# Two stages of a hybrid layer become one block: the whole output product in 32 units of pieces, with a ring of weight slots

## What is computed

```
attn = sliding_window_attention(q, k, v, sinks) * silu(z_attn)
...
y = ssd_chunked(xs, dt, a, bm, cm)
y = y + (xs.reshape(b, l, N_SSM_HEADS, SSM_HEAD_DIM) * d_skip[:, None]).reshape(b, l, D_INNER)
ssm = gated_rmsnorm(y, z_ssm, ssm_norm_w)
out = jnp.einsum("ble,ed->bld", jnp.concatenate([attn, ssm], axis=-1), w_out)
return layer_norm_2(DEEPNORM_ALPHA * x + out, ln_g, ln_b)
```

## Time and profile before

| | us |
|---|---|
| median of 3 runs | 3448.87 (3447.88 to 3450.91) |
| profiled execution, its own time | 3451.71 |
| its span, first to last instruction | 3449.8 |
| layer 0: state-space block | 2146.2 to 2400.4 |
| layer 0: `state_out_and_norm`, last product | 2400.4 to 2498.05 |
| layer 1: the same | 3087.1 to 3341.5, 3341.5 to 3439.9 |
| mean granted TensorE clock | 0.953 |

### The profile page before, as it was taken

The page is one execution under the profiler, slowest core; times in us unless marked ns, Lnnn a source line. Parts: engine busy times, 40 slices in busy tenths (PEclk is TensorE's granted clock), DMA queues, the critical chain, the costliest instruction groups (busy, mean ns, idle before and its releaser), DMA issues. The chain is left out here.

```text
span 3449.8 us, 49680 instructions
## 1 busy us (share of the span) xinstructions
PE 3145.1 (91%) x21066; PEld 2491.3 (72%) x21066; DVE 1482.6 (43%) x2152; ACT 1061.8 (31%) x1832; POOL 996.3 (29%) x658
## 2 busy tenths in 40 slices
PE   5998799785999998998999998788999999978888
PEld 3886498674888887887777776566777777756667
DVE  3999644434222224342243342554412433425544
ACT  3012333323222222222243443541213444444411
POOL 2443022103333323322333332221323333321212
PEclk8999799897999999999999999899999999988999
DMA  5113300122111111123111222653331112226432
GB/s 199 49 49 116 105 4 4 44 100 93 47 48 49 49 36 52 60 95 100 50 61 62 74 86 91 217 147 104 114 86 50 62 62 74 92 104 204 144 113 102
DMA packets 296327, 292.82 MB, mean 85 GB/s; under 512 B 10784, under 2 KB 252832, under 8 KB 291648
## 3 DMA queue, kind: packets, MB, share of 16 engines
q1 hardware_dynamic: 252320, 235.28, 21.5%
q10 hardware_dynamic: 43808, 54.66, 4.6%
HBM read 233.16 MB, written 54.66 MB: 83 GB/s over the span
## 5 line engine op out<-in xcount | busy, mean ns | idle before, releaser
L1880 PE MATMUL PS<-x_high_sb,w_high_sb 128*128 128x512 f32 x1312 | 530.1, 404 | 0.0
L1880 PE MATMUL PS<-x_high_sb,w_low_sb 128*128 128x512 f32 x1312 | 518.2, 395 | 0.0
L1880 PE MATMUL PS<-x_low_sb,w_high_sb 128*128 128x512 f32 x1312 | 517.4, 394 | 0.0
L1880 PEld LDWEIGHTS PS<-x_high_sb,w_high_sb 128*128 128x128 f32 x1312 | 246.9, 188 | 76.1 <-issue 23.9
L1880 PEld LDWEIGHTS PS<-x_high_sb,w_low_sb 128*128 128x128 f32 x1312 | 246.8, 188 | 57.8
L360 PE MATMUL PS<-h_high_sb,up_high_sb 128*128 128x512 f32 x704 | 274.7, 390 | 14.1 <-POOL up_low_sb L1445 14.1
L1880 PEld LDWEIGHTS PS<-x_low_sb,w_high_sb 128*128 128x128 f32 x1312 | 247.3, 188 | 52.4
L360 PE MATMUL PS<-h_low_sb,up_high_sb 128*128 128x512 f32 x704 | 274.6, 390 | 0.0
L360 PE MATMUL PS<-h_high_sb,up_low_sb 128*128 128x512 f32 x704 | 274.4, 390 | 0.0
L1495 DVE SCALAR_TENSOR_TENSOR z_sb<-PS,cols_sb,z_sb 128x1023 f32<-128x1023 f32 x88 | 112.8, 1282 | 348.5 <-ACT z_sb L1476 342.1
L2118 DVE CUSTOM_DVE_ANT_0 scores_sb<-PS,alibi_sb,sinks_sb 128x256 f32<-128x256 f32 (+1 forms) x256 | 104.4, 465 | 342.5 <-PE PS L1898 342.5
(11 more groups left out here) (414 smaller groups left out, 6316.6 us busy)
## 6 DMA issues: line engine op xcount, KB each, us to landing
w_raw_sb<-w_in SPq DMA_DIRECT2D x102, 512.0 KB, 3.8
up_raw_sb<-w_up SPq DMA_DIRECT2D x44, 512.0 KB, 3.8
ada_slots_sb<-ada_w SPq DMA_DIRECT2D x16, 1024.0 KB, 5.9
attn_raw_sb<-attn ACTq DMA_DIRECT2D x32, 512.0 KB, 4.7
decays_sb<-running_sums SPq DMA_DIRECT2D x16, 1024.0 KB, 5.2
w_raw_sb<-w_out SPq DMA_DIRECT2D x64, 256.0 KB, 3.5
xbc<-staged_sb ACTq DMA_DIRECT2D x24, 512.0 KB, 2.6
xbc_sb<-xbc SPq DMA_DIRECT2D x16, 768.0 KB, 6.9
```

Source lines behind the costliest of these rows:

```text
L1880: last = pe.matmul(PS[:, bank, :], a[:, n % 2, k], b[:, k, cols], start=k == 0 and a is WH and b is HH, stop=k == KT - 1 and a is WL)
```

## The change

The two blocks become one, `state_space_and_mix`. The output product has 32 units in four parts of 8: attention rows with the left columns, attention rows with the right columns, ssm rows left, ssm rows right. Units 0 and 1 run ahead of chunk 0, two units in each chunk, units 18 and 19 around the last norm, and 20 to 31 behind it. Units 0 to 17 share one PSUM bank, the later ones take four in turn. The ssm units read y from HBM in the same layout as the attention units. The weights of all 32 pieces pass through a ring of 11 slots (`WS`), and a slot is filled again when the last unit of a part has used its piece (`slot_empty`). The first 8 pieces are loaded into the room of y and state by two transfers and split by ScalarE and VectorE (`first`) at the block's start; pieces 8 to 31 are split by GpSimd, in three runs between the `grow` passes. SyncE issues pieces 10 to 12 in chunk 1, 13 to 20 in chunk 2, 21 to 26 in chunk 6, and the last 5 into the room of y and state. The z gate has one buffer where it had two, so `gates(c)` waits for `gate(c - 1)`. The squares go to y's own room. The norm weight is multiplied in `normalise`, now 8 passes of 128 columns. The layer norm is what it was.

```diff
@@ -2175,7 +2175,9 @@
-def state_space_and_attention_out(m, d_skip, xbc_d, gate_d, rows_d, attn_d, y_d, src, w, DT, A, NA, EI, DE, CD):
+def state_space_and_mix(m, layer, d_skip, xbc_d, gate_d, rows_d, attn_d, y_d, src, w, ln_g, ln_b, dst, ahead,
+                        DT, A, NA, EI, DE, CD):
...
@@ -2183,34 +2185,39 @@
-    SLOTS = 3
-    UNITS = 2 * TT
+    SLOTS, WS = 3, 11
+    UNITS, FREE = 4 * TT, 2 * TT + 2
...
-        ZS = alloc(m, ctx, "z_gate", [P, 2, KT, P])
+        ZS = alloc(m, ctx, "z_gate", [P, KT, P])
...
+        YS = alloc(m, ctx, "y_and_state", [P, 4, DI])
...
+        WH = alloc(m, ctx, "w_high", [P, WS, NH], F32R)
+        WL = alloc(m, ctx, "w_low", [P, WS, NH], F32R)
+        Y, S = YS[:, 0:2], YS[:, 2:4]
+        raw = YS[:].rearrange("p a (b n) -> p (a b) n", n=NH)
...
@@ -2218,6 +2225,23 @@
+        bank = lambda u: OUT if u < FREE else (u - FREE) % 4
+        before = lambda u: u if u < FREE else u - 3
+        LATE, RESIDUAL = [4, 5, 6, 7, 0], [0, 1, 4, TT]
+        late = lambda i: i - (4 * KT - len(LATE))
...
+        def slot_empty(eng, i):
+
+            j, q = (i - WS) // KT, (i - WS) % KT
+            if q == KT - 1:
+                eng.wait_ge(s.prod, TT * (j + 1))
+            else:
+                eng.wait_ge(s.piece, (KT - 1) * j + q + 1)
@@ -2232,42 +2256,46 @@
...
             def gates(c):
-                sp.dma_start(ZS[:, c % 2], chunk(gate_d[:, :, cols(c)])).then_inc(z_in[c % 2], 16)
+                if c:
+                    sp.wait_ge(s.gate, c)
+                sp.dma_start(ZS[:], chunk(gate_d[:, :, cols(c)])).then_inc(s.z_in, 16)
...
+            def first_weights(i):
+                sp.dma_start(raw[:, 4 * i:4 * i + 4], w[4 * i * P:4 * (i + 1) * P, 0:NH].rearrange("(q p) n -> p q n", p=P)
+                             ).then_inc(first_in[i], 16)
+
+            def piece_of(i):
+                part, q = i // KT, i % KT
+                row, half = part // 2 * KT + q, part % 2
+                return w[row * P:(row + 1) * P, half * NH:(half + 1) * NH]
 
             def weights(i):
-                if i >= 2:
-                    sp.wait_ge(s.wsplit, i - 1)
-                half, q = i // KT, i % KT
-                sp.dma_start(RAW[:, i % 2], w[q * P:(q + 1) * P, half * NH:(half + 1) * NH]).then_inc(raw_in[i % 2], 16)
+                if i >= KT + 2:
+                    sp.wait_ge(s.wsplit, i - KT - 1)
+                sp.dma_start(RAW[:, i % 2], piece_of(i)).then_inc(raw_in[i % 2], 16)
 
             def store(c):
                 sp.wait_ge(s.normed, c + 1)
                 sp.dma_start(chunk(y_d[:, :, cols(c)]), YT[:, c % 2]).then_inc(y_out[c % 2], 16)
 
             inputs(0)
+            sp.dma_start(skip[:], d_skip.to_broadcast([P, SH])).then_inc(s.skip_in, 16)
+            first_weights(0)
+            first_weights(1)
+            residual(0)
             rows(0)
-            weights(0)
-            weights(1)
-            sp.dma_start(skip[:], d_skip.to_broadcast([P, SH])).then_inc(s.skip_in, 16)
+            residual(1)
             rows(1)
-            weights(2)
             inputs(1)
-            weights(3)
-            residual(0)
-            weights(4)
-            rows(2)
-            weights(5)
-            gates(0)
-            weights(6)
-            residual(1)
-            weights(7)
-            gates(1)
             weights(8)
             weights(9)
+            rows(2)
+            gates(0)
+            residual(2)
             for c in range(TT):
                 sp.wait_ge(s.yd, c + 1)
-                if c == 4:
-                    for i in range(10, 2 * KT):
-                        weights(i)
+                for i in {1: range(10, 13), 2: range(13, 21), 6: range(21, 27)}.get(c, ()):
+                    weights(i)
                 if c:
                     store(c - 1)
-                    if c + 1 < TT:
-                        gates(c + 1)
+                    gates(c)
+            sp.wait_ge(s.yo, TT - 1)
+            sp.wait_ge(s.ss, TT - 1)
+            for i in range(4 * KT - len(LATE), 4 * KT):
+                sp.dma_start(raw[:, LATE[late(i)]], piece_of(i)).then_inc(s.tail_in, 16)
+                if i == 4 * KT - len(LATE):
+                    store(TT - 1)
...
@@ -2294,19 +2331,23 @@
+                    i = u // TT * KT + q
                     if q == 0:
                         pe.wait_ge(s.low, u + 1)
-                        if u:
-                            pe.wait_ge(s.added, u)
+                        if u and before(u):
+                            pe.wait_ge(s.added, before(u))
                     if k == 0:
-                        pe.wait_ge(s.wsplit, half * KT + q + 1)
+                        if i < KT:
+                            pe.wait_ge(s.wfirst, i + 1)
+                        else:
+                            pe.wait_ge(s.wsplit, i - KT + 1)
...
@@ -2396,80 +2438,106 @@
 
             b_and_cb(0)
             x_turned(0)
+            fill(2 * KT)
             for c in range(TT):
-                n = 1 if c else 0
                 if c + 1 < TT:
                     b_and_cb(c + 1)
-                fill(n)
+                fill(1)
                 if c:
                     from_state(c)
-                else:
-                    fill(4)
-                fill(2 * n)
+                fill(2)
                 if c < TT - 1:
                     to_state(c)
                 fill(2)
                 if c:
                     y_turned(c - 1)
-                fill(2 * n)
+                fill(2)
                 within(c)
-                fill(1 if c else 2)
+                fill(1)
                 if c + 1 < TT:
                     x_turned(c + 1)
-                fill(3 * n)
+                fill(3)
                 if c:
                     square_sums(c - 1)
-                fill(3 * n)
+                fill(3)
                 if c:
                     spread(c - 1)
-                fill(2 * n)
+                fill(2)
             y_turned(TT - 1)
-            fill(4)
+            pe.wait_ge(s.xde, TT)
+            fill(KT)
             square_sums(TT - 1)
-            fill(4)
+            fill(KT)
             spread(TT - 1)
+            fill(len(pieces))
...
             def split(i):
-                half, q = i // KT, i % KT
...
+                if late(i) >= 0:
+                    pool.wait_ge(s.tail_in, 16 * len(LATE))
+                    piece = raw[:, LATE[late(i)]]
+                else:
+                    pool.wait_ge(raw_in[i % 2], 16 * (i // 2 - KT // 2 + 1))
+                    piece = RAW[:, i % 2]
+                if i >= WS:
+                    slot_empty(pool, i)
+                nc.gpsimd.tensor_copy(WH[:, i % WS], piece).then_inc(s.wchain, 1)
+                pool.wait_ge(s.wchain, i - KT + 1)
+                nc.gpsimd.tensor_tensor(WL[:, i % WS], piece, WH[:, i % WS], ALU.subtract).then_inc(s.wsplit, 1)
...
-                if c == 5:
-                    for i in range(KT, 2 * KT):
-                        split(i)
+
+            pool.wait_ge(s.wfirst, KT)
+            for i in range(KT, WS):
+                split(i)
+            for c in range(1, 4):
+                grow(c)
+            for i in range(WS, WS + KT):
+                split(i)
+            for c in range(4, TT - 1):
+                grow(c)
+            for i in range(WS + KT, 4 * KT):
+                split(i)
...
             load(0)
+            load(1)
             move(0)
+            high(0)
+            for i in range(KT):
+                first(i)
             act.wait_ge(s.kept, 1)
             floors(0)
             exps(0)
-            high(0)
             high(1)
             floors(1)
             exps(1)
+            high(2)
             for c in range(TT):
+                a = 2 * c + 2
                 if c + 1 < TT:
                     move(c + 1)
-                if c:
-                    high(2 * c)
+                high(a + 1)
                 if c + 2 < TT:
                     floors(c + 2)
                 if c:
                     square(c - 1)
                 if c + 2 < TT:
                     exps(c + 2)
+                high(a + 2)
                 if c:
-                    high(2 * c + 1)
                     root(c - 1)
             square(TT - 1)
+            high(FREE + 1)
             root(TT - 1)
+            act.wait_ge(s.kept, 4)
+            act.wait_ge(s.yd, TT)
+            for u in range(FREE + 2, UNITS):
+                high(u)
+                if u >= UNITS - TT + 2:
+                    norm(u - (UNITS - TT + 2))
...
+            def first(i):
+                dve.wait_ge(s.whigh, i + 1)
+                v.tensor_tensor(WL[:, i], raw[:, i], WH[:, i], ALU.subtract).then_inc(s.wfirst, 1)
...
             def normalise(c):
                 dve.wait_ge(s.spread, 2 * c + 2)
-                h = YT[:, c % 2].rearrange("p (g k) n -> p g k n", g=SG)
```

(22 more changed lines are left out.)

282 lines of the change are left out of this document (100 added, 182 removed).

## The result

The changed kernel takes **3470.8 us** (median of 4 runs, 3466.8 to 3472.7) where the kernel before takes 3448.4 beside it: 1.0062 of it, with a 95% interval of 1.0045 to 1.0079. It is slower by 22 us; the forecast was 3447 us and the range ended at 3464.

What follows compares the result with a forecast made beforehand. TensorE, busy for 91% of the span, was taken to bound the kernel; 58.8 + 206.9 + 85.3 = 351.0 us a layer against 351.9, so two layers give 2 us: 3447 us from a median of 3448.87, range 3429 to 3464.

Steps and rivals of the forecast that it cites:

- rival of the ring's last pieces: Last five weight pieces, behind the last turn of y: slower GpSimd splits make piece 31 late; about 3457 us, chance 0.27.
- slower side: Outcome slower than the kernel before by over 0.2% (7 us): chance 0.27.
- rival of shorter queue stalls: Weight pieces land sooner than forecast in chunk 1 and for gates(2): 3425 to 3437 us, chance 0.28.
- chunk 7: Pieces 21 to 26 hold back gates(6), so y's addition is late: 1.5 us a layer with latencies.
- Part 3: Last turn of y to the last product: 85.3 us a layer, 25.7 less than before.
- Part 1: Block start to chunk 1: 58.8 us a layer, 8.1 more than before, for three more units done.
- chunk 1 over a regular one: grow(1) stands behind the split of late piece 10: 17.0 us and 2.4 of half clock, 19.4 a layer.
- chunk 3 over a regular one: gates(2) is held back behind weight pieces up to 18: 7.1 us and 2.2 of clock, 9.3 a layer.
- normalisation: Eight passes of 128 columns for one of 1,024: 0.25 us by seven chunks, 1.75 a layer.
- rest of Part 2: Chunks 1 to 7 as six regular periods and a last one without a product on the state: 174.9 us.
- Part 2: Chunks 1 to 7, up to the last turn of y: 206.9 us a layer, 16.7 more than before.
- clock term: Open end of the range for the clock: -3 to +3 us a layer.

Runs made afterwards that it cites:

- e1: Changed kernel with GpSimd's grow(1) listed ahead of the split of piece 10, grow(2) and grow(3) right behind it: 3432.3 us, ratio 0.9952.
- e8: Changed kernel with gates(6) alone moved ahead of pieces 21 to 26 and of store(5): 3462.6 us.
- e7: Changed kernel with the gated normalisation in one VectorE pass in place of eight, the norm weights left out: 3465.2 us, ratio 1.0042.
- e9: e6 with unit 2's tile asked for ahead of the casts of the first weights, and exps(0) ahead of high(2): 3376.4 us, ratio 0.9783.
- e10: Changed kernel with gates(7) alone moved ahead of store(6): 3460.8 us, ratio 1.0033.
- e12: Changed kernel with the layer norm's rows asked for behind gates(6) and the next layer's first weights behind the first store of the result: 3468.0 us.
- e4: Changed kernel with the edits of e1, e2 and e3 together: 3389.7 us, ratio 0.9824.
- e6: Changed kernel with e1, a fuller reordering of the start, z gates ahead (chunk 2's behind piece 13), next layer's first weights behind the first store: 3384.2 us.
- e11: Changed kernel with the decay rows rows(0) asked for second in SyncE's queue in place of fifth: 3468.3 us.
- e2: Changed kernel with SyncE's gates(c) of chunks 2 to 7 ahead of that chunk's weight pieces and store(c - 1): 3437.4 us, ratio 0.9968.
- e3: Changed kernel with ScalarE's high(1) ahead of floors(0), and VectorE's low(1) and add(0) ahead of the skip diagonal: 3464.7 us.

## Why the prediction was wrong

**The frame held.** TensorE's work stayed the same; the 12.6 us between the blocks went, and new waits took their place where the prediction put them: unit 1 at the start, piece 10 ahead of `grow(1)` (12.7 and 4.05 us of idle time where "some 12" and 4 were forecast), the z gate of chunks 3 and 7, no gap between the blocks. The rival of the ring's last pieces (3457) did not come about: two of layer 0's five subtractions took 2.15 and 2.27 us in place of 1.28, but the five splits took 11.5 us, not 14.3, and TensorE waits 0.8 to 1.9 us for them. So the slower side, which had a chance of 0.27, came about for other reasons than its own. The rival of shorter queue stalls did not either: piece 10 was ready 7.4 us after its issue (2222.72 to 2230.12; before, 7.2). The Trainium skill (DMA: Bandwidth & Descriptors, Anatomy of one DMA) gives about 2.0 us plus the bytes at 436 GB/s for a transfer that GpSimd issues, an estimated 2.6 us for a piece. SyncE's piece that moves alone took 2.5, close to it; one behind rows and xbc took almost three times that.

**The step that failed is the sizing of three terms of the sum, each about 4 us short in layer 0**: "chunk 7: 1.5"; Part 3's 85.3, which priced idle time without half clock and did not have the wait for unit 23's tile; and in Part 1 the landing of the first decay rows. Term by term, in us of one layer (layer 0, and layer 1 behind the stroke):

| term | forecast | measured | by |
|---|---|---|---|
| Part 1 | 58.8 | 62.8 / 61.3 | windows |
| chunk 1 over a regular one | 19.4 | 18.9 / 19.3 | trace; e1 |
| chunk 3 over a regular one | 9.3 | 10.2 / 10.3 | trace |
| chunk 7 | 1.5 | 5.4 / 5.0 | e8 |
| normalisation | 1.75 | 3.1 (0.44 x 7) | trace; e7 |
| rest of Part 2 | 174.9 | 175.9 / 175.8 | remainder |
| Part 3 | 85.3 | 89.4 / 88.9 | windows |

- *Chunk 1 and chunk 3*, the two large terms, were within 1 us, and e1 confirms the first in a run: 38.5 us for twice 19.4. (The passes listed for the two chunks add up to 19.1 and 32.7 us where the prediction writes 18.95 and 32.4; it changes nothing.)
- *Chunk 7*: I had `gates(6)` issued 15.2 us after unit 15 begins. It was issued 18.3 us after (2400.57 against about 2382.3), since six pieces took 14.7 us from the first issue to the last. That makes TensorE's wait 4.8 us in place of 2.8 (1.5 on top of the 1.3 that stays in e8), and I had given a wait of this size no half clock, though its window shows a granted clock of 0.58 for 4.7 us.
- *Part 3*: in e9's tail, at full clock throughout, TensorE is busy for 79.98 us, which is the forecast's 77.0 + 2.9. The changed kernel's is busy for 83.0 and idle for 6.4. So 3.1 us are half clock, of which I had none, and 1.0 is idle time beyond my 5.4. The wait for `gates(7)` was not the mis-sized part: I had 2.9 + 1.5 = 4.4 for it, all idle time, and e10 gives back 4.1 in layer 0, 2.6 of idle time and 1.5 of half clock. Wholly absent from the sum was unit 23's tile of y, held back by transfers that the same stretch asks for; taking them away gives 1.3 us in e12 and 3.0 where the z gate is on time (e4 to e6).
- *Part 1*: `rows(0)` landed 19.1 us after the block's start; I had 15.8 from the bytes ahead of it in the queue. What is asked for right behind it moves at the same time. That is argued from the transfers' order; e11, which moved it ahead, shows that its place is paid for by the first weights. Chunk 0 took 22.0 us where I had 20.6, and this contains the wait for xbc ahead of chunk 1, 1.15 us, which I had called covered; where that wait is missing (layer 1, e1), chunk 0 takes 20.7 to 20.8.
- *Normalisation*: a pass of 128 columns took 0.27 us (2.15 for eight) in place of the estimated 0.22, and all of the surplus fell on the path. The 1.0 us in the rest of Part 2 is in chunk 7, where the last turn of y also waits 0.76 us for the eight passes.

The errors were 12.7 and 14.7 us a layer, 27 in all, less the 4.5 us by which the rest was shorter in the profiled execution. None was large, and all but chunk 1's had one sign. The range had a clock term of -3 to +3 a layer, as if it could be won as well as lost; in these traces half clock follows idle time, so each new wait that I named should have carried its own.

**What the change itself is worth** is seen in e9: with the same blocks, ring and units, and the lists reordered, 3376 us. In the change as made, the gain between the blocks (21.6 us a layer in Part 3) is outweighed by what Parts 1 and 2 add (12.1 and 23.3), mostly queued passes; Part 1 also does three more units.

**Open:** whether rows of decay land late because of what is behind them was not measured by itself, nor what bounds the start at 54 us. The changed kernel's runs spread over 6 us against 3 before, and its layer 1 tail varies by 5 us between kernels that do not touch it; neither has an explanation here.

## What to carry to other kernels

When passes with unlike urgency share an engine's in-order list, look for each at the one ahead of it and at what that one waits for: here a pass of 1.9 us on the state, and a tile of 0.5 MB, each queued behind weights that nobody needed yet, cost 72 us between them. Price a wait with the clock behind it, and carry it through to the next unit, since a stall taken out at one place came back in part at the next in three of the runs (e2, e3, e12). And before packing more work into a start, work out its bytes at the mean rate of a well-packed start: here that gave 54 us, which the two best orders of the lists reached and none passed.

## What the hardware showed that I had not expected

A transfer's issue can itself hold the queue's engine for long. SyncE's 38 issues of weight pieces, shortest, median and longest in ns, and when the first and the last were made:

```profile
L2279 SPq DMA_DIRECT2D w_raw_sb<-w_out x38: 327/328/13163, 2153.6 to 3351.9; - x38
```

The longest, 13.2 us with no semaphore to wait for, is one at the block's start, behind nine other transfers of its queue and two of ScalarE's. `rows(2)`, `gates(0)` and the last residual stood behind it; in the kernel before the longest issue of a piece in this block was 1.4 us. In e9 the hold falls on `residual(1)`, behind seven transfers of its queue: 11.6 us. No run here took this wait away by itself, so its price is not known.
